# One tile's layers moved four picks up, three of its steps held back behind the expert sums, and one wait added on the weight queue

## The chip, the cores and the metric

One Trainium2 chip, one core of it. The metric is device time in microseconds (us) of one execution. A measurement of this kernel can tell about 0.2% from no change.

## The reference

256 tokens of width 1024 pass through two blocks. The first ends in a retrieval feed-forward: each token sums 128 expert rows (8 heads, 16 picks each), with a dot product against one half of a row and a weighted sum of the other half. The second block is a layer stack (short convolution, memory attention, gate/up/down feed-forward, block attention, the same again, a final norm). Cut to what matters here:

```python
def peer_ffn(h, w_query, sub_keys, expert_u, expert_v):      # per block of 128 tokens
    ...
    u = expert_u[experts]
    vsel = expert_v[experts]
    act = jax.nn.gelu(jnp.einsum('thkd,td->thk', u, hb), approximate=False)
    return jnp.einsum('thk,thkd->td', gate * act, vsel)

def swiglu(h, w_gu, w_down):
    g, u = jnp.split(h @ w_gu, 2, axis=-1)
    return (jax.nn.silu(g) * u) @ w_down

for l in range(DEPTH_2):                                       # second block, two layers
    x = x + (short_conv_mixer or moba_attention)(rms_norm_2(x, norm_mix[l]), ...)
    x = x + mem_cross_attention(rms_norm_2(x, norm_mem[l]), ...)
    x = x + swiglu(rms_norm_2(x, norm_ffn[l]), ffn_w_gu[l], ffn_w_down[l])
```

## The kernel before

The 256 tokens are two tiles of 128. The experts are worked in 256 **picks**, one per step n of a ring: picks 0 to 127 belong to tile 0, picks 128 to 255 to tile 1. A pick is one gather by GpSimd of 128 rows of 8 KB (one row for each partition, 1 MiB in all, L1646) into one of nine places (`SLOTS = 9`); a dot product on VectorE (L2145); gelu, weight and a small diagonal matrix on ScalarE (L1592, L1598, L1605); and its sum on TensorE (L1172). Picks go in pairs, so four matmuls of L1172 (written x8 by the trace, which counts two passes of an f32 matmul) are one pair. The gather of pick n waits until `v_used`, the count of summed picks, has reached n - 8.

Under the second half of the picks TensorE does other work: when tile 0's sums are complete (`add_experts(0)`, L2151 to L2161, on VectorE), tile 0's layers run between the pairs of tile 1. Which step stands before which pair is the table `PICK_WORK`, filled by the loop over `STEPS` from pick `LAYER_FIRST` on. `UNDER_ROWS` are the steps of tile 0 placed there. The rest of them (before: the six down products `dn1` and the final norm) is put between steps of tile 1 after the last pair, by the table `FILLS`, which makes `AFTER_ROWS`. All engines walk the same tables, each doing its own part of a step. On VectorE the dots of a pair stand ahead of its part of the step placed one pair earlier, so a dot can wait behind a product of TensorE.

A product step (`gu1 10`, say: the last of eleven gate/up products of the second feed-forward) is 8 matmuls of 128x512 with one 2 MB block of weights (L1011; down products L1089), after which ScalarE and VectorE empty the bank. A turn (`fturn1 4`) is up to four transposes of 128x128 (L1018). `fturn1 4` turns what `gu1 8` and `gu1 9` made, `fturn1 5` what `gu1 10` made.

SyncE asks for the weight blocks in the order of use (`SEQUENCE`), into a ring of three places (`RING_B = 3`): a block is asked for when the product that used the place three blocks before is done (`wait_released`, L607). So the weights of a step are asked for three products ahead, and gathers and weight blocks share the DMA engines. At the last pairs the order is `gu1 8`, `gu1 9`, `gu1 10` of tile 0, then `dn1 0` of tile 0, then `cin 2` of tile 1.

Of the kernel before, what the change touches and what calls it, by code (L numbers as in the profile page):

```python
# [27 lines left out]
PH, PN, PK = 8, 128, 16  # L28
# [8 lines left out]
SLOTS = 9  # L37
# [160 lines left out]
def memory_steps(l):  # L198

    return [(f"turn mem{l}", 2, 2), (f"root mem{l}", 0, 0), (f"q{l} 0", 7, 2), (f"q{l} 1", 7, 0), (f"qturn{l} 0", 2, 2), (f"scores{l} 0", 4, 2),  # L200
            (f"probs{l} 0", 0, 2), (f"pturn{l} 0", 2, 2), (f"values{l} 0", 4, 2), (f"mo{l} 0", 7, 2), (f"mo{l} 1", 7, 0)]


def feed_steps(l):

    steps = [(f"turn ffn{l}", 2, 2), (f"root ffn{l}", 0, 0)]
    for j in range(11):
        steps.append((f"gu{l} {j}", 7, 0 if j else 2))
        if j >= 2 and j % 2 == 0:
            steps.append((f"fturn{l} {j // 2 - 1}", 1, 0))  # L210
    return steps + [(f"fturn{l} 5", 1, 2)] + [(f"dn{l} {c}", 7, 0 if c else 2) for c in range(6)]
# [4 lines left out]
         + [("turn blk", 2, 2), ("root blk", 0, 0), ("bk 0", 7, 2), ("bk 1", 7, 0), ("bq 0", 7, 0), ("bq 1", 7, 0), ("bv 0", 7, 0), ("rope 0", 0, 0),  # L216
            ("bv 1", 7, 0), ("kturn 0", 2, 2), ("bqturn 0", 2, 0), ("bscores 0", 2, 2), ("bprobs 0", 0, 2), ("bpturn 0", 2, 2), ("bvalues 0", 3, 2),
            ("bo 0", 7, 2), ("bo 1", 7, 0)] + memory_steps(1) + feed_steps(1) + [("final 0", 0, 2)])
LAYER_FIRST, PICK_US = 136, 5.2
UNDER_ROWS, DOWN = [], [f"dn1 {c}" for c in range(6)]  # L220
_at, _load = LAYER_FIRST, float(LAYER_FIRST)
for _w, _us, _lag in STEPS:
    _at = max(_at + _lag, 2 * int(_load // 2))
    _load = max(_load, _at) + _us / PICK_US
    if _w not in DOWN + ["final 0"]:
        assert _at < 256
        UNDER_ROWS.append(_w)
        PICK_WORK.setdefault(_at, []).append("layer 0 " + _w)
FILLS = {"turn conv": ["dn1 0"], "cin 2": ["dn1 1"], "pturn0 0": ["dn1 2"], "bk 0": ["dn1 3"], "bpturn 0": ["dn1 4"], "pturn1 0": ["dn1 5"],
         "gu1 3": ["final 0"]}  # L230
AFTER_ROWS = []
for _w, _us, _lag in STEPS:
    for _fill in FILLS.get(_w, ()):
        AFTER_ROWS += [(0, "gain 0")] * (_fill == "final 0") + [(0, _fill)]
# [58 lines left out]
def unit(name):  # L293
    return [n for n, _ in UNITS].index(name)
# [27 lines left out]
def build_program(nc, a, out):  # L322
    plan = weight_plan(a)
    piece = {}
    for n, (name, i, _) in enumerate(plan):
        piece[name, i] = n

    with ExitStack() as ctx:
# [5 lines left out]
        def sem(name):  # L334
            if name not in sems:
                sems[name] = ctx.enter_context(nc.semaphore(name))
            return sems[name]
# [159 lines left out]
        for n in range(len(plan)):  # L497
            i = n % RING if n < RING_4 else EARLY_PLACES[n - RING_4] if n < RING_4 + len(EARLY_PLACES) else (n - RING_4 - len(EARLY_PLACES)) % RING_B
# [14 lines left out]
        dots_done, v_used = sem("dots_done"), sem("v_rows_used")  # L513
# [43 lines left out]
        def wait_released(eng, n):  # L557

            name, i, _ = plan[n]
            if name == "mod":  # L560
                eng.wait_ge(turn_ready, turn(f"m{i}") + 1)
            elif (name, i) == ("out", 0):
                eng.wait_ge(sem("out_half_used"), 1)
            elif (name, i) in last_unit:
                eng.wait_ge(unit_ready, unit(last_unit[name, i]) + 1)
            else:
                eng.wait_ge(sem("piece_used"), middle.index((name, i)) + 1)
# [9 lines left out]
        @block.sync  # L577
        def _(sp):
            sp.dma_start(keep[:, 0:K_COS], a["keep"][:, 0:K_COS]).then_inc(sem("consts_in"), 16)
            for n, (name, i, parts) in enumerate(plan):  # L580
                if n == 3:
                    sp.dma_start(mem[1], a["ctxT"]).then_inc(sem("ctxT_in"), 16)
                    sp.dma_start(small_rows, a["small_rows"]).then_inc(sem("small_rows_in"), 16)
                    sp.dma_start(keep[:, K_COS:K_END], a["keep"][:, K_COS:K_END]).then_inc(sem("late_consts_in"), 16)
                if n == 5:
                    in4 = piece["in", 4]
                    sp.dma_start(slot8[slot_of[in4]][:, 4:8], plan[in4][2][0][0][:, 4:8]).then_inc(landed[slot_of[in4]], 32)
                    sp.dma_start(s_all[:, 0:2048], a["dist"]).then_inc(sem("dist_in"), 16)
                if n == 8:
                    sp.wait_ge(sem("lam_sums"), 1)  # L590
                    sp.dma_start(x, a["x"][0].rearrange("(t p) d -> p t d", p=P)).then_inc(sem("x_in"), 16)
                if (name, i) == ("wq", 0):
                    sp.wait_ge(unit_ready, unit("c1k1") + 1)
                    sp.dma_start(mem[1], a["skT"]).then_inc(sem("keys_in"), 16)
                if (name, i) == ("mk0", 0):
                    sp.wait_ge(sem("h2_ready"), 4)
                    sp.dma_start(mem[2], a["memT"]).then_inc(sem("mem_in"), 16)
                if user_before[n] is not None:
                    wait_released(sp, user_before[n])
                if n == piece["in", 4]:  # L600
                    sp.dma_start(slot8[slot_of[n]][:, 0:4], parts[0][0][:, 0:4]).then_inc(sem("in4_first_half"), 16)
                    continue
                for src, c0, c1 in parts:
                    dst = ring[:, slot_of[n] * 4096 + c0:slot_of[n] * 4096 + c1]
                    if len(src.shape) == 3:
                        dst = dst.rearrange("p (k n) -> p k n", k=src.shape[1])
                    sp.dma_start(dst, src).then_inc(landed[slot_of[n]], 32 // len(parts))  # L607
            for t in range(NT):
                for u, c in enumerate((slice(0, 512), slice(512, D))):
                    sp.wait_ge(sem(f"tile{t}_done{u}"), 1)  # L610
                    sp.dma_start(out[0].rearrange("(t p) d -> p t d", p=P)[:, t, c], x[:, t, c]).then_inc(sem("stored"), 16)
            sp.wait_ge(sem("stored"), 64)
# [1039 lines left out]
        def _(dve):  # L1652
# [3 lines left out]
            def link(ins):  # L1656

                n_steps[0] += 1
                ins.then_inc(steps, 1)
                dve.wait_ge(steps, n_steps[0])  # L1660
# [195 lines left out]
            for half in range(2):  # L1856
                c = slice(half * 512, (half + 1) * 512)
# [290 lines left out]
            def add_experts(t):  # L2148

                dve.wait_ge(v_used, 128 * (t + 1))  # L2150
                acc = (M, T)[t]  # L2151
                for half in range(2):
                    c = slice(half * 512, (half + 1) * 512)
                    part = (h2[:, 0], expert_part)[t][:, c]
                    if half == 0:
                        link(tt(part, acc[0][:, :], g5row[:, c], ALU.mult))
                    else:
                        for to, at in ((0, 64), (64, 0)):
                            q = tt(part[to:to + 64], acc[1][at:at + 64, :], g5row[at:at + 64, c], ALU.mult)
                        link(q)  # L2160
                    tt(x[:, t, c], x[:, t, c], part, ALU.add).then_inc(experts_added[t], 1)  # L2161
# [14 lines left out]
            def memory_scale(l):  # L2176

                if l:
                    dve.wait_ge(sem("mem_sd"), 1)
                    link(nc.vector.reciprocal(rs_m, rs_m))  # L2180
                for k in range(KC):
                    g = C_MKV + 8 * l + k
                    q = stt(memT[l][:, k], memT[0][:, k], cols[:, g:g + 1], rs_m, ALU.mult, ALU.mult)
                q.then_inc(sem("mem_scaled"), 1)
# [7 lines left out]
                    (2, 0): [lambda: key_copy(0, 5), lambda: key_copy(1, 5)],  # L2192
                    (2, 1): [lambda: key_copy(0, 6), lambda: key_copy(1, 6)], (2, 3): [lambda: key_copy(0, 7), lambda: key_copy(1, 7)],
                    (3, 1): [set_ones], (3, 3): [memory_mean],
                    (4, 0): [lambda: memory_scale(1)], (4, 1): [lambda: memory_scale(0)], (8, 1): [lambda: add_experts(0)]}
            tri = keep[:, K_TRI:K_TRI + P]

            def layer_step(t, step, arg):
# [207 lines left out]
```

## Time and profile before

| | |
|---|---|
| runs | 1719.26, 1721.23, 1718.58 us (median 1719.26) |
| profiled execution, its span | 1719.4 us; the page gives no other time of it |
| TensorE busy | 1520.7 us, 88% |
| VectorE, ScalarE, GpSimd busy | 44%, 29%, 17% |
| bytes moved by DMA | 586.83 MB, 341 GB/s over the span |

Times in the trace run from the span's start. A line of the timeline is a run of like instructions on one engine: start, length, line, what it writes and reads, how many, and in brackets the idle time before it with what ended it. The windows give busy time of each engine in a stretch, the clock granted to TensorE (1.00 is full speed) and the rate of the DMA engines. In the list of DMA queues, q0 carries the gathers and q1 the weight blocks.

### The profile page before, as it was taken

To read this page: it belongs to the slowest core of one execution; us is meant where nothing else is said; L and a number is where in the kernel's file an instruction comes from. 1 tells how busy PE (TensorE), PEld (TensorE's weight loads), DVE (VectorE), ACT (ScalarE), POOL (GpSimd) and SP (SyncE) were. 2 spreads that over 40 slices of the span, in tenths; PEclk is the share of its full clock that TensorE was granted. 3 is DMA by queue.
4 is the path that set the end of the run, shared out by engine and by line. 5 is a ranking of instruction groups with operands and counts; after the bars stand their busy time and mean duration, and the time that the engine had idled before them with its cause. 6 is when DMAs were issued, how large, how long until landed. Compare 5 with 4: busy or idle time off the path is not lost.

```text
span 1719.4 us, 15639 instructions
## 1 busy us (share of the span) xinstructions
PE 1520.7 (88%) x5502; PEld 730.4 (42%) x5502; DVE 752.0 (44%) x1816; ACT 502.0 (29%) x1284; POOL 292.4 (17%) x264
## 2 busy tenths in 40 slices
PE   8999998685489894997999897899999999999998
PEld 5444463462153530333343333443444444455443
DVE  2853178866786566456435436532312100031101
ACT  2412134332433223333443224443412110122210
POOL 0000003434434243223212213321000000000000
PEclk9999999896589896898999998899999999999999
DMA  9736339999999999999999999999876677855774
GB/s 371 257 122 227 140 125 406 403 421 421 421 402 421 421 421 421 399 421 420 415 422 419 422 421 420 413 421 422 347 296 235 259 298 284 306 219 217 289 299 185
DMA packets 94029, 586.83 MB, mean 341 GB/s; under 512 B 6912, under 2 KB 7168, under 8 KB 28288
## 3 DMA queue, kind: packets, MB, share of 16 engines
q1 hardware_dynamic: 56080, 313.19, 46.7%
q0 software_dynamic: 37440, 270.55, 38.1%
q10 hardware_dynamic: 432, 2.10, 0.3%
q8 instruction: 44, 0.72, 0.2%
q14 instruction: 33, 0.27, 0.0%
HBM read 584.76 MB, written 1.05 MB: 341 GB/s over the span
## 4 chain that ended last, share of the span: by engine, by line
PE 71%; DMA 18%; DVE 5%; issue 3%; ACT 2%; POOL 0%; SPq 0%; POOLq 0%; DVEq 0%; ACTq 0%
PE bank L1011 34%; DMA arena<-in_peer_rows,pidx 10%; DMA ring<-in_weights 8%; PE bank L1089 7%; PE bank L701 7%; PE bank L1172 4%; PE bank L779 3%; PE bank L976 2%; DVE arena L2145 2%; PE bank L1018 2%; PE bank L987 2%; PE bank L667 1%; PE bank L756 1%; PE bank L1071 1%; DMA ring<-in_w_mod 1%
## 5 line engine op out<-in xcount | busy, mean ns | idle before, releaser
L1646 POOL DMA_INDIRECT arena<-in_peer_rows,pidx x227 | 257.4, 1134 | 578.2 <-PE bank L1172 531.3
L2145 DVE SCALAR_TENSOR_TENSOR arena<-arena,ring 128x1024 f32<-128x1024 f32 x227 | 273.2, 1223 | 111.9 <-DMA arena<-in_peer_rows,pidx 109.1
L1011 PE MATMUL bank<-ring,arena 128*128 128x512 f32 x736 | 319.4, 593 | 0.0
L1011 PE MATMUL bank<-ring,hT_all 128*128 128x512 f32 x544 | 244.4, 605 | 15.6 <-issue 10.6
L1172 PE MATMUL bank<-arena,keep 128*32 128x512 f32 x908 | 159.8, 704 | 101.1 <-ACT keep L1605 101.1
L1011 PEld LDWEIGHTS bank<-ring,arena 128*128 128x128 f32 x736 | 138.5, 190 | 168.8 <-issue 168.7
L1011 PEld LDWEIGHTS bank<-ring,hT_all 128*128 128x128 f32 x544 | 102.8, 193 | 150.9 <-issue 140.2
L1592 ACT ACTIVATE pf<-pf 128x2 f32<-128x2 f32 x128 | 25.9, 202 | 401.4 <-DVE arena L2145 367.1
L2266 DVE TENSOR_TENSOR x_all<-x_all,bank 128x512 f32<-128x512 f32 x40 | 27.5, 688 | 209.6 <-PE bank L1089 115.8
L1172 PEld LDWEIGHTS bank<-arena,keep 128*32 128x32 f32 x908 | 21.3, 115 | 171.1 <-ACT keep L1605 135.0
L701 PE MATMUL bank<-ring,hT_all 128*128 128x512 f32 x192 | 86.0, 603 | 0.6 <-DVE hT_all L1725 0.6
L1646 POOL DMA_INDIRECT spare<-in_peer_rows,pidx x29 | 32.4, 1118 | 296.9 <-DVE pidx L2068 205.4
L1089 PE MATMUL bank<-ring,arena 128*128 128x512 f32 x176 | 75.9, 592 | 0.0
L2289 DVE SCALAR_TENSOR_TENSOR arena<-bank,stat,arena 128x256 f32<-128x256 f32 x22 | 10.6, 484 | 136.2 <-ACT arena L1550 136.2
L1605 ACT ACTIVATE keep<-keep,pf 128x32 f32<-128x32 f32 x256 | 68.2, 313 | 4.2
L779 PE MATMUL bank<-hT_all,ring 128*128 128x128 f32 (+1 forms) x384 | 61.6, 320 | 3.3 <-DMA ring<-in_weights 2.5
L1089 PE MATMUL bank<-ring,s_all 128*128 128x512 f32 x128 | 58.5, 611 | 6.6 <-DMA ring<-in_weights 6.6
L1598 ACT ACTIVATE pf<-pf,grouped 128x1 f32<-128x1 f32 x256 | 61.4, 287 | 4.4
L976 PE MATMUL bank<-mem_all,ring 128*128 128x256 f32 x256 | 62.6, 402 | 0.0
L779 PEld LDWEIGHTS bank<-hT_all,ring 128*128 128x128 f32 x384 | 55.6, 198 | 12.2 <-issue 5.8
L987 PE MATMUL bank<-ring,mem_all 128*128 128x512 f32 x128 | 58.3, 602 | 0.0
L976 PEld LDWEIGHTS bank<-mem_all,ring 128*128 128x128 f32 x256 | 50.5, 201 | 18.0 <-issue 9.2
(391 smaller groups left out, 1698.2 us busy)
## 6 DMA issues: line engine op xcount, KB each, us to landing
ring<-in_weights SPq DMA_DIRECT2D x122, 2048.0 KB
ring<-in_w_mod SPq DMA_DIRECT2D x12, 2048.0 KB
ring<-in_w_in SPq DMA_DIRECT2D x5, 2048.0 KB
ring<-in_weights SPq DMA_DIRECT2D x8, 1024.0 KB
ring<-in_weights SPq DMA_DIRECT2D x8, 512.0 KB
arena<-in_peer_rows,pidx POOLq DMA_INDIRECT x227
ring<-in_w_in SPq DMA_DIRECT2D x2, 1024.0 KB, 17.6
mem_all<-in_b_mod POOLq DMA_DIRECT2D x3, 512.0 KB, 7.2
```

The source lines that it names most:

```text
L701: m = mm(b[:, :], src[:, k, t * P:(t + 1) * P], slot8[w][:, k], start=(k == 0), stop=(k == KC - 1))
L779: m = mm(b[:, s * n:(s + 1) * n], slot8[w][:, k, c:c + P], hT[:, k, cols_of], start=(k == 0), stop=(k == KC - 1))
L976: m = mm(bk[:, b * TOK:(b + 1) * TOK], slot8[w][:, k, (2 * half + b) * P:(2 * half + b + 1) * P], memT[l][:, k], start=(k == 0), stop=(k = ...
L987: m = mm(b[:, :], memT[l][:, 4 * part + k, t * P:(t + 1) * P], slot4[w][:, k, half * 512:(half + 1) * 512], start=(part == 0 and k == 0), ...
L1011: m = mm(b[:, :], src[:, k], slot8[w][:, k], start=(k == 0), stop=(k == KC - 1))
L1018: i = tr(b[:, c * P:(c + 1) * P], src, ident)
L1089: m = mm(b[:, :], v.fT[k], slot8[w][:, k % 8], start=(k == ks[0]), stop=(k == ks[-1]))
L1172: m = mm(acc[b][r:r + 32, :], diag[n % 8], vslot[n % SLOTS][:, b * 512:(b + 1) * 512], start=(n % 128 < 4), stop=(n % 128 >= 124))
L1598: m = f(pw2[:, c + k:c + k + 1], pgel2[:, c + k:c + k + 1], ACT.Copy, scale=grouped[:, g % 4, i % 4, 1, i // 4:i // 4 + 1])
L1605: f(diag[n % 8], eq32, ACT.Copy, scale=pw2[:, c + k:c + k + 1]).then_inc(sem("diag_ready"), 1)
L1646: nc.gpsimd.indirect_dma_start(out=row_in[n % SLOTS], out_offset=None, in_=a["peer_rows"], in_offset=bass.IndirectOffsetOnAxis(ap=pidx[:, ...
L2145: stt(uslot[n % SLOTS], uslot[n % SLOTS], 1.0, h2g[n % 4], ALU.mult, ALU.mult, accum_out=pact2[:, 16 * (g % 2) + k:16 * (g % 2) + k + 1]). ...
```

## The change

1. `LAYER_FIRST` goes from 136 to 132: every step of tile 0 that stays under the picks stands four picks earlier (the first, `turn conv`, ahead of pick 134 in place of 138).
2. `add_experts(0)` on VectorE, which those steps need, moves from behind the dots of pair 134 to behind those of pair 130.
3. `gu1 10`, `fturn1 4` and `fturn1 5` of tile 0 leave the picks and run after the last pair. The fills between tile 1's steps are dealt out anew: `gu1 10` and `fturn1 4` ahead of tile 1's first turn, `fturn1 5` and `dn1 0` ahead of its `cin 2`, and `dn1 1`, `dn1 2` one place later than before; a place at `gu0 0` is new. The last step of tile 0 under the picks, `gu1 9`, stands ahead of pair 244 in place of pair 248.
4. SyncE waits until 247 picks are summed before it asks for `dn1 0` of tile 0 and, its queue being in order, for all that follows.

```diff
-LAYER_FIRST, PICK_US = 136, 5.2
-UNDER_ROWS, DOWN = [], [f"dn1 {c}" for c in range(6)]
+LAYER_FIRST, PICK_US = 132, 5.2
+UNDER_ROWS, DOWN, HELD = [], [f"dn1 {c}" for c in range(6)], ["gu1 10", "fturn1 4", "fturn1 5"]
...
-    if _w not in DOWN + ["final 0"]:
+    if _w not in DOWN + HELD + ["final 0"]:
...
-FILLS = {"turn conv": ["dn1 0"], "cin 2": ["dn1 1"], "pturn0 0": ["dn1 2"], "bk 0": ["dn1 3"], "bpturn 0": ["dn1 4"], "pturn1 0": ["dn1 5"],
-         "gu1 3": ["final 0"]}
+FILLS = {"turn conv": ["gu1 10", "fturn1 4"], "cin 2": ["fturn1 5", "dn1 0"], "pturn0 0": ["dn1 1"], "gu0 0": ["dn1 2"], "bk 0": ["dn1 3"],
+         "bpturn 0": ["dn1 4"], "pturn1 0": ["dn1 5"], "gu1 3": ["final 0"]}
...
+                if (name, i) == ("dn10", 0):
+                    sp.wait_ge(v_used, 16 * PK - SLOTS)
...
-                    (4, 0): [lambda: memory_scale(1)], (4, 1): [lambda: memory_scale(0)], (8, 1): [lambda: add_experts(0)]}
+                    (4, 0): [lambda: memory_scale(1)], (4, 1): [lambda: memory_scale(0)], (8, 0): [lambda: add_experts(0)]}
```

TensorE at the end of the picks, before: from `fturn1 3` (L1018 x4, ahead of `gu1 9` and pair 248) to the first product after the last pair, `dn1 0` (L1089). Rows of L1172 are pairs.

```order
L1018 MATMUL bank<-keep,s_all 128x128 x4
L1011 MATMUL bank<-ring,hT_all 128x512 x8
L1172 MATMUL bank<-arena,keep 32x512 x4
L1011 MATMUL bank<-ring,hT_all 128x512 x8
L1018 MATMUL bank<-keep,s_all 128x128 x4
L1172 MATMUL bank<-arena,keep 32x512 x4
L1018 MATMUL bank<-keep,s_all 128x128 x2
L1172 MATMUL bank<-spare,keep 32x512
L1172 MATMUL bank<-arena,keep 32x512
L1172 MATMUL bank<-spare,keep 32x512
L1172 MATMUL bank<-arena,keep 32x512 x5
L1089 MATMUL bank<-ring,s_all 128x512 x8
```

The same place in the changed kernel (its lines are two higher: L1174 is the pairs, L1013 and L1091 the products, L1020 the turns), from `fturn1 3` on.

```order
L1020 MATMUL bank<-keep,s_all 128x128 x4
L1013 MATMUL bank<-ring,hT_all 128x512 x8
L1174 MATMUL bank<-arena,keep 32x512 x16
L1174 MATMUL bank<-spare,keep 32x512
L1174 MATMUL bank<-arena,keep 32x512
L1174 MATMUL bank<-spare,keep 32x512
L1174 MATMUL bank<-arena,keep 32x512 x5
L1013 MATMUL bank<-ring,hT_all 128x512 x8
L1020 MATMUL bank<-keep,s_all 128x128 x4
L1020 MATMUL bank<-keep,x_all 128x128 x8
L1020 MATMUL bank<-keep,s_all 128x128 x2
L1091 MATMUL bank<-ring,s_all 128x512 x8
```

Before, `gu1 9` was followed by four pairs (248 to 254) with `gu1 10` and two turns among them; now it is followed by six pairs (244 to 254) with nothing among them, and `gu1 10`, the two turns and tile 1's first turn (x8) follow the last pair.

VectorE around `add_experts(0)`, before (L2145 are dots, L2156 to L2161 are `add_experts(0)`; the rest chooses rows of later picks):

```order
L2009 MAX_INDEX ptop<-pf,s_all 128x8
L2145 SCALAR_TENSOR_TENSOR arena,pf<-arena,ring 128x1024
L2145 SCALAR_TENSOR_TENSOR spare,pf<-spare,ring 128x1024
L2156 TENSOR_TENSOR h_all<-bank,hT_all 128x512
L2161 TENSOR_TENSOR x_all<-x_all,h_all 128x512
L2159 TENSOR_TENSOR h_all<-bank,hT_all 64x512 x2
L2161 TENSOR_TENSOR x_all<-x_all,h_all 128x512
L2014 CAST pf<-ptop 128x32
```

And in the changed kernel (L2147 are the dots, L2158 to L2163 `add_experts(0)`):

```order
L1687 COPY ring<-bank 128x512 x4
L2147 SCALAR_TENSOR_TENSOR arena,pf<-arena,ring 128x1024 x4
L2158 TENSOR_TENSOR h_all<-bank,hT_all 128x512
L2163 TENSOR_TENSOR x_all<-x_all,h_all 128x512
L2161 TENSOR_TENSOR h_all<-bank,hT_all 64x512 x2
L2163 TENSOR_TENSOR x_all<-x_all,h_all 128x512
L2007 MAX pf<-s_all 128x8
```

The work of `add_experts(0)` is the same; it stands two pairs of dots earlier, right behind the dots of picks 128 to 131.

## Rows read from the trace of the kernel before

**Rows 1.** The page: chain that ended last, by engine and line.
```profile
PE 71%; DMA 18%; DVE 5%; issue 3%; ACT 2%; POOL 0%; SPq 0%; POOLq 0%; DVEq 0%; ACTq 0%
```

**Rows 2.** Windows: stretch, busy PE, PEld, DVE, ACT, POOL, then PEclk, DMA share, GB/s.
```profile
900.00:1100.00 200.00, 173.41 (x568) 73.68 (x567) 100.03 (x239) 68.10 (x186) 47.33 (x44) 0.92 1.01 419
1180.00:1225.00 45.00, 43.30 (x129) 17.66 (x128) 11.70 (x23) 21.36 (x42) 5.18 (x5) 1.00 1.01 422
1250.00:1719.00 469.00, 456.75 (x1287) 219.95 (x1286) 70.70 (x159) 76.25 (x161) 0.00 (x0) 1.00 0.70 264
```

**Rows 3.** Timeline of TensorE at the end of the picks.
```profile
1202.32 1.06 PE L1172 MATMUL bank<-arena,keep 128*32 128x512 f32 x8
1203.64 7.13 PE L1011 MATMUL bank<-ring,hT_all 128*128 128x512 f32 x16 [0.25 <-DMA ring<-in_weights]
1210.70 1.06 PE L1172 MATMUL bank<-arena,keep 128*32 128x512 f32 x8
...
1212.19 7.03 PE L1011 MATMUL bank<-ring,hT_all 128*128 128x512 f32 x16
1219.15 1.06 PE L1172 MATMUL bank<-arena,keep 128*32 128x512 f32 x8
1220.15 7.13 PE L1011 MATMUL bank<-ring,hT_all 128*128 128x512 f32 x16
...
1231.97 1.07 PE L1172 MATMUL bank<-arena,keep 128*32 128x512 f32 x8 [1.89 <-ACT keep L1605]
1232.96 7.13 PE L1089 MATMUL bank<-ring,s_all 128*128 128x512 f32 x16
```

**Rows 4.** Timeline of GpSimd: the gathers of picks 253, 254 and 255.
```profile
1204.18 1.19 POOL L1646 DMA_INDIRECT arena<-in_peer_rows,pidx  x1 [14.65 <-PE bank L1172]
1205.67 0.93 POOL L1646 DMA_INDIRECT arena<-in_peer_rows,pidx  x1 [0.30 <-issue]
1212.56 0.94 POOL L1646 DMA_INDIRECT arena<-in_peer_rows,pidx  x1 [5.95 <-PE bank L1172]
```

**Rows 5.** DMA queues in 1106 to 1126: packets, MB, share of 16 engines.
```profile
q0 software_dynamic: 1150, 8.37, 100.7%
```

**Rows 6.** DMA queues in 1203 to 1208.
```profile
q1 hardware_dynamic: 273, 2.11, 101.0%
q0 software_dynamic: 1, 0.00, 0.0%
```

**Rows 7.** DMA queues in 1208 to 1210.
```profile
q1 hardware_dynamic: 62, 0.50, 59.8%
q0 software_dynamic: 42, 0.34, 41.4%
```

**Rows 8.** DMA queues in 1182 to 1200.
```profile
q1 hardware_dynamic: 507, 3.91, 52.1%
q0 software_dynamic: 497, 3.68, 49.1%
```

**Rows 9.** DMA queues in 1223 to 1224, where the gathers' last packets are.
```profile
q1 hardware_dynamic: 49, 0.38, 90.4%
q0 software_dynamic: 10, 0.04, 10.0%
```

**Rows 10.** Timeline of VectorE: the last product's copy and the last dots.
```profile
1227.83 0.48 DVE L2289 SCALAR_TENSOR_TENSOR s_all<-bank,stat,s_all 128x256 f32<-128x256 f32 x1 [5.29 <-ACT s_all L1550]
1228.23 1.22 DVE L2145 SCALAR_TENSOR_TENSOR arena<-arena,ring 128x1024 f32<-128x1024 f32 x1
```

**Rows 11.** Timeline of VectorE at tile 0's first steps.
```profile
671.70 1.22 DVE L2145 SCALAR_TENSOR_TENSOR arena<-arena,ring 128x1024 f32<-128x1024 f32 x1 [1.18 <-DMA arena<-in_peer_rows,pidx]
...
684.12 1.22 DVE L2145 SCALAR_TENSOR_TENSOR arena<-arena,ring 128x1024 f32<-128x1024 f32 x1
...
693.44 0.69 DVE L2206 TENSOR_TENSOR hT_all<-bank,keep 128x512 f32<-128x512 f32 x1
```

**Rows 12.** Timeline of TensorE at tile 0's first steps.
```profile
674.30 1.93 PE L1172 MATMUL bank<-arena,keep 128*32 128x512 f32 x8 [3.27 <-ACT keep L1605]
...
686.72 1.94 PE L1172 MATMUL bank<-arena,keep 128*32 128x512 f32 x8 [5.50 <-ACT keep L1605]
688.59 1.73 PE L1018 MATMUL bank<-keep,x_all 128*128 128x128 f32 x8
...
694.23 16.93 PE L1011 MATMUL bank<-ring,hT_all 128*128 128x512 f32 x32 [2.57 <-issue]
```

**Rows 13.** Chain in order of time, tile 1's last products: start, us, what.
```profile
1659.56 0.44 PE bank L1018 x4
1659.99 13.75 PE bank L1011 x32
...
1674.82 0.44 PE bank L1018 x2
```

## The prediction

> **What bounds the kernel now.** I read the chain of the whole span first [rows 1]: TensorE holds 71% of it and DMA 18%, so there are stages of two kinds. The windows tell them apart [rows 2]. From 900 to 1100 us the DMA engines are full (share 1.01, 419 GB/s) while TensorE is busy 173 of 200 us: under the picks, bytes set the pace. From 1250 to the end TensorE is busy 456.75 of 469 us and DMA 70%: there TensorE sets it. Between them, from about 1203 us, lies a short stretch in which TensorE hardly rests either: 43.3 of 45 us [rows 2]. The end of the kernel is therefore (the moment of the last pair) + (all that is left for TensorE). Before, the last pair ends and `dn1 0` starts at 1232.96 [rows 3], and 1719.4 - 1233.0 = 486.4 us follow. I work out how the change moves both.
>
> The timeline of the last pairs shows what they wait for [rows 3]. Pair 244 is summed at 1202.32, then come `gu1 8`, pair 246, a turn, `gu1 9` (1212.19 to 1219.15), pair 248, `gu1 10`, and the rest. The gathers of 253 and 254 are issued 0.8 us after pair 244 is summed, that of 255 after pair 246 [rows 4].
>
> **Part 1, four picks earlier: a gain of 9.6 us at the last step under the picks.** Tile 0's steps keep their order and the pairs between them, and four gathers fewer go ahead of each. With only gathers in flight, 8.37 MB took 20 us [rows 5], so a gather of 1.049 MB is worth 2.5 us and four are worth 10.0, as long as DMA stays full. At the start VectorE decides instead: it is busy throughout, and the first copy of tile 0 stands behind the dots that begin at 684.12 in place of those that end just ahead of 693.44 [rows 11]. That copy then starts at 684.1 + 1.2 = 685.3, and 1.2 us earlier still, since `add_experts(0)` now fills the wait of 1.18 us ahead of 671.70: 684.1, or 9.3 us earlier. TensorE's own wish would be 12.4 us (688.59 - 676.2, the end of pair 132 in place of that of pair 136) [rows 12]. I take 9.6, between 9.3 and 10.0, and keep 8 and 12.4 as ends. So `gu1 9` should be done at 1219.15 - 9.6 = 1209.6.
>
> **Part 2, the last pairs with nothing between them.** This is where the gain is spent. Behind `gu1 9` there now stand six pairs in place of four. Pair 244, which let the gathers of 253 and 254 go ahead of `gu1 8`, now comes behind `gu1 9`. It ends at 1209.6 + 1.0 = 1210.6, and the first of the last three gathers is issued at 1211.4, where before it was 1204.2: in spite of the 9.6 us gained, 7.2 us later.
>
> Before, from that issue to the last byte of pick 255 it took 19.4 us: issued at 1204.18 [rows 4]; up to 1208 not a byte moves on the gathers' queue, which has one packet, while the weights' queue takes all [rows 6]; in the next 2 us there are 0.34 MB [rows 7]; and the last 0.04 MB pass between 1223 and 1224 [rows 9]. So some 4.3 us to the first byte and 15 us for three gathers, 5 us each. That they take 5 and not 2.5 us is the sharing: with both queues full each gets half, 3.68 MB against 3.91 in 18 us [rows 8]. The new wait does not end this. It opens at 247 summed, which is pair 246, right behind pair 244. SyncE then asks for `dn1 0` and at once for `cin 2`, whose place `gu1 9` has freed. 4 MB of weights so run beside the last three gathers from their first byte on. I take the same 19.4 us: pick 255 has landed at 1230.8. (Alone, the three would need 7.5 us in place of 15; I keep that for a rival.)
>
> From the landing to the last sum: before, the dots of 254 and 255 waited behind the copy of `gu1 10` [rows 10], and the last sums ended 4.7 us after the first of them began. With no product in the way only one dot remains. From the start of the dots at 1228.23, two dots of 1.15 us each end at 1230.55, the sums begin at 1231.97 and end at 1232.96 [rows 3]: so 1.4 us pass on ScalarE and 1.0 us on TensorE. One dot, with some 0.3 us ahead of it for the semaphore (my estimate), makes it 0.3 + 1.2 + 1.4 + 1.0 = 3.9 us. With a slow TensorE the sums take 1.94 in place of 1.07 [rows 12]: 4.8 us. End of the picks: 1230.8 + 4.8 = 1235.6, **2.6 us later than before**.
>
> **Part 3, what is left after the last pair: 7.6 us more.** One product is 13.75 / 2 = 6.9 us, `fturn1 4` 0.44 and `fturn1 5` at most 0.44 [rows 13], and none of them replaces a wait: that stretch is busy to 97% [rows 2]. The moved fills cost nothing. `fturn1 5` needs the copy of `gu1 10`, ready about 1 us behind it, and the turns between them take 0.44 + 0.9 us. `gu1 10` itself covers `add_experts(1)` as `dn1 0` did. The new place ahead of `gu0 0` covers a wait of under 1 us. The blocks asked for late (`dn1 0`, `cin 2`) land by about 1233 (3.2 MB of their 4.2 beside the gathers, the rest at full rate), while `dn1 0` is needed 8.7 us behind the last pair and `cin 2` 15.6 us behind it, so I set the added wait at nothing too. If that cover were gone it would cost up to 5 us, one block at full rate.
>
> **Part 4, the clock: 3.0 us more.** From about 1212 to 1235 TensorE would have only four pairs to sum, with gaps of 5 to 10 us. After a gap of 5.5 us before, a pair took 1.94 us, and the products that followed took 16.93 us for two [rows 12] where two take 13.75 at full clock [rows 13]. The granted clock was 1.00 in the stretch of the last pairs before [rows 2]; it should fall to the lower of its two levels (1.2 of 2.4 GHz) and `gu1 10` should pay the difference of 3.2 us, less a little for the first turns being among the slow work: 3.0. The lower end is nothing, if the clock holds.
>
> **Sum:** 2.6 + 7.6 + 3.0 = 13.2 us, against the profiled execution of 1719.4: 1732.6. The median of the runs is 1719.26, 0.1 lower, so **1732.5 us**, 0.8% slower. With the ends of the unknown terms: shift 12.4, no loss of clock (-2.8 - 3.9) gives 1725.9; shift 8 (+1.6) and two of the last gathers 1 us slower each gives 1736.2.
>
> A rule of the Trainium skill would soften this. The page "DMA: Bandwidth & Descriptors", section "Latency and other measured facts", puts the first byte of a DMA issued by GpSimd at about 1 us. The rows here show 4.3 us for a gather. By the page, pick 255 would land 3.3 us earlier and the sum would be 1729.2.
>
> **Rivals.**
> 1. *The last gathers run alone (faster).* The place is the same: gathers 253 to 255 behind `gu1 9`. If weights asked for at pair 246 start too late to take their share, the three need 7.5 us: pick 255 in at 1211.4 + 4.3 + 7.5 = 1223.2, last pair done 1227.1 at full clock, end -5.9 + 7.6 = +1.7. With the shift of 12.4 it is -1.1, and with a quicker first byte (rival 2) -4.4: 1715. It decides when pick 255 lands before 1221.5 (1233.0 - 7.6 - 3.9), 10.1 us behind the issue of 253. For it speaks that the weights' queue needs time too; against it that it is asked 1 us behind and gave half from the start in [rows 7]. Faster over all: 0.12. The part of it that ends within 0.2%, 1716 to 1722.7: 0.10.
> 2. *The first byte comes sooner.* The gather's 4.3 us could be the price of a queue found busy by 2 MB of weights; where the queues are nearly empty, as they now are behind `gu1 10`'s block, it might be 1 us. The time is 1729, within my range. 0.10, slower.
> 3. *Late blocks.* `dn1 0` or `cin 2` lands late and tile 1 starts behind: up to 5 us on top, 1737.6. 0.08.
> 4. *The forecast* (nothing but the sum, 1725.9 to 1736.2): 0.60.
>
> That the change does not do what it says is ruled out by the order of the instructions.
>
> **How the numbers follow.** Slower by over 0.2%: 0.60 + 0.10 + 0.08 = 0.78; within 0.2% (1715.8 to 1722.7, about what a measurement can tell): 0.10; faster: 0.12. The range leaves out the faster case and most of the late blocks: 1718 to 1736.
>
> **What the changed profile would show.** `turn conv`'s first product at 685 in place of 694.2; `gu1 9` done near 1209.6; a stretch of some 25 us behind it with only pairs and a granted clock of 0.5; the gather of 253 issued near 1211; the last byte of gathers near 1231; `gu1 10` beginning at 1235.6 and taking about 10 us; from there to the end 497 us. I am wrong if gathers 253 to 255 land within 12 us of their issue, if `gu1 9` is done before 1205, or if TensorE keeps its clock.

## The result, and the profile after

The changed kernel takes 1733.15 us (median of 4 runs, 1731.88 to 1734.51), the kernel before 1720.24 (4 runs). The ratio is 1.0074, with a 95% interval of 1.006 to 1.0087: slower by 0.7%. Forecast were 1732.5 us and slower. The profiled execution has a span of 1730.1 us (that same execution is timed at 1731.9), 10.7 more than before. In every run on record whose execution has both figures the timed one is 1.7 to 1.9 us above the span, so the profiled execution before, of 1719.4, stands for about 1721.2 us. It was therefore 1.0 us slower than the median of its four, and that of the changed kernel 1.3 us faster than the median of its own: that is why the spans differ by 10.7 us and the medians by 12.9.

The windows of the changed kernel, with the columns of [rows 2]:

```profile
900.00:1100.00 200.00, 167.37 (x564) 72.59 (x564) 106.45 (x259) 69.92 (x195) 51.21 (x47) 0.94 1.01 419
1180.00:1225.00 45.00, 33.20 (x114) 11.70 (x112) 13.46 (x24) 15.43 (x36) 9.29 (x7) 0.84 0.96 384
1209.00:1234.00 25.00, 7.45 (x48) 0.90 (x39) 9.90 (x17) 6.16 (x22) 5.16 (x3) 0.60 0.76 305
1250.00:1730.00 480.00, 467.46 (x1313) 224.83 (x1311) 72.08 (x161) 76.25 (x161) 0.00 (x0) 1.00 0.70 263
```

The stages on both sides look as before: full DMA under the picks, 97% of TensorE after them. The stretch between them does not. TensorE was busy 43.3 of 45 us there and is now busy 33.2; from 1209 to 1234 it works 7.45 of 25 us, at a mean clock of 0.60, and DMA is not full either.

The timeline of TensorE in that stretch answers to [rows 3] (lines are two higher; the pair between 1215 and 1233 is printed in single rows and left out):

```profile
1201.47 7.03 PE L1013 MATMUL bank<-ring,hT_all 128*128 128x512 f32 x16
1208.43 1.92 PE L1174 MATMUL bank<-arena,keep 128*32 128x512 f32 x16
1213.18 1.28 PE L1174 MATMUL bank<-arena,keep 128*32 128x512 f32 x8 [2.83 <-ACT keep L1607]
1215.48 1.94 PE L1174 MATMUL bank<-arena,keep 128*32 128x512 f32 x8 [1.02 <-ACT keep L1607]
...
1233.05 1.93 PE L1174 MATMUL bank<-arena,keep 128*32 128x512 f32 x8 [7.81 <-ACT keep L1607]
1234.91 8.55 PE L1013 MATMUL bank<-ring,hT_all 128*128 128x512 f32 x16
```

`gu1 9` ends at 1208.4 (before: 1219.15), the last pair at 1234.9 (before: 1232.96). So 10.7 us are gained up to `gu1 9`, and 12.7 are lost between it and the last pair. The gathers say why. GpSimd, as in [rows 4]:

```profile
1210.28 1.19 POOL L1648 DMA_INDIRECT arena<-in_peer_rows,pidx  x1 [6.12 <-PE bank L1174]
1211.77 1.99 POOL L1648 DMA_INDIRECT arena<-in_peer_rows,pidx  x1 [0.30 <-issue]
1214.07 1.98 POOL L1648 DMA_INDIRECT arena<-in_peer_rows,pidx  x1 [0.30 <-issue]
```

They are those of 253, 254 and 255, the first 6.1 us later than before. The chain in order of time then ends the picks:

```profile
1214.07 16.36 DMA arena<-in_peer_rows,pidx
1230.42 0.02 issue
1230.44 1.24 DVE arena L2147 x2
...
1233.05 1.93 PE bank L1174 x8
1234.98 8.48 PE bank L1013 x16
```

Pick 255 has landed at 1230.4, 20.1 us after the issue of 253. The list of DMA queues from 1215 to 1229 shows what passed beside the three gathers, to compare with [rows 8]:

```profile
q1 hardware_dynamic: 390, 3.00, 50.9%
q0 software_dynamic: 390, 2.93, 49.8%
```

Half and half. And from 1211 to 1214, where SyncE had asked for two blocks at 1210.4 and the gathers had not begun:

```profile
q1 hardware_dynamic: 93, 0.76, 85.0%
```

### The profile page after: what moved, and what is told of

Its sections match the earlier page's. It is cut to its first block, busy times and chain, and to the rows that moved or that the text cites. A ratio compares the mean times of both kernels' runs of the same rounds, so it can differ in the third digit from the quotient of the medians.

```text
span 1730.1 us, 15642 instructions
## 1 busy us (share of the span) xinstructions
PE 1521.4 (88%) x5502; PEld 729.3 (42%) x5502; DVE 752.5 (43%) x1816; ACT 502.9 (29%) x1285; POOL 293.4 (17%) x264
## 4 chain that ended last, share of the span: by engine, by line
PE 67%; DMA 23%; DVE 5%; issue 2%; ACT 2%; POOL 0%; POOLq 0%; SPq 0%; DVEq 0%; ACTq 0%
PE bank L1013 33%; DMA arena<-in_peer_rows,pidx 11%; DMA ring<-in_weights 9%; PE bank L1091 7%; PE bank L703 7%; PE bank L1174 4%; PE bank L781 2%; PE bank L978 2%; DMA spare<-in_peer_rows,pidx 2%; PE bank L1020 2%; DVE arena L2147 2%; PE bank L989 1%; PE bank L669 1%; PE bank L758 1%; DMA ring<-in_w_mod 1%
## 5 line engine op out<-in xcount | busy, mean ns | idle before, releaser
L2147 DVE SCALAR_TENSOR_TENSOR arena<-arena,ring 128x1024 f32<-128x1024 f32 x227 | 273.7, 1223 | 131.5 <-DMA arena<-in_peer_rows,pidx 128.6
L1013 PE MATMUL bank<-ring,arena 128*128 128x512 f32 x736 | 319.3, 593 | 0.0
L1013 PE MATMUL bank<-ring,hT_all 128*128 128x512 f32 x544 | 249.2, 615 | 19.3 <-issue 10.5
L1174 PE MATMUL bank<-arena,keep 128*32 128x512 f32 x908 | 161.8, 715 | 104.7 <-ACT keep L1607 104.7
L1013 PEld LDWEIGHTS bank<-ring,arena 128*128 128x128 f32 x736 | 138.6, 190 | 169.1 <-issue 169.0
L1013 PEld LDWEIGHTS bank<-ring,hT_all 128*128 128x128 f32 x544 | 104.7, 197 | 159.3 <-issue 145.4
L1174 PEld LDWEIGHTS bank<-arena,keep 128*32 128x32 f32 x908 | 21.7, 115 | 176.3 <-ACT keep L1607 137.8
L703 PE MATMUL bank<-ring,hT_all 128*128 128x512 f32 x192 | 86.0, 603 | 0.6 <-DVE hT_all L1727 0.6
L1091 PE MATMUL bank<-ring,arena 128*128 128x512 f32 x176 | 75.9, 592 | 0.0
L2291 DVE SCALAR_TENSOR_TENSOR arena<-bank,stat,arena 128x256 f32<-128x256 f32 x22 | 10.7, 484 | 138.4 <-ACT arena L1552 138.4
L1091 PE MATMUL bank<-ring,s_all 128*128 128x512 f32 x128 | 58.4, 610 | 5.1 <-DMA ring<-in_weights 5.1
## 6 DMA issues: line engine op xcount, KB each, us to landing
ring<-in_w_in SPq DMA_DIRECT2D x2, 1024.0 KB, 17.4
```

What stands on the lines that cost most here:

```text
L703: m = mm(b[:, :], src[:, k, t * P:(t + 1) * P], slot8[w][:, k], start=(k == 0), stop=(k == KC - 1))
L1013: m = mm(b[:, :], src[:, k], slot8[w][:, k], start=(k == 0), stop=(k == KC - 1))
L1091: m = mm(b[:, :], v.fT[k], slot8[w][:, k % 8], start=(k == ks[0]), stop=(k == ks[-1]))
L1174: m = mm(acc[b][r:r + 32, :], diag[n % 8], vslot[n % SLOTS][:, b * 512:(b + 1) * 512], start=(n % 128 < 4), stop=(n % 128 >= 124))
L2147: stt(uslot[n % SLOTS], uslot[n % SLOTS], 1.0, h2g[n % 4], ALU.mult, ALU.mult, accum_out=pact2[:, 16 * (g % 2) + k:16 * (g % 2) + k + 1]). ...
```

## The experiments

Profiled executions of kernels that are alike up to pick 240 differ by up to 3.8 us in when they reach tile 0's first product (682.6 in the changed kernel, 686.3 and 686.4 in the first two runs below), so I read each run from three marks of its timeline: the end of `gu1 9`, the end of the last pair, and the end of the span. The last column is the ratio of the run times to those of the kernel before, taken on the same chip. A profiled execution can lie off its median (that of two picks and the wait 2.5 us below, that of two picks without it 2.7 below), so the marks show where time goes and the ratio what a kernel is worth.

| kernel | `gu1 9` ends | last pair ends | between | from there to the end | span | ratio, 95% |
|---|---|---|---|---|---|---|
| before | 1219.2 | 1233.0 | 13.8 | 486.4 | 1719.4 | |
| changed | 1208.4 | 1234.9 | 26.5 | 495.2 | 1730.1 | 1.0074 (1.006 to 1.0087) |
| without the wait | 1211.2 | 1236.7 | 25.5 | 494.5 | 1731.2 | 1.008 (1.0058 to 1.0101) |
| wait for all 256 | 1210.8 | 1228.2 | 17.4 | 494.7 | 1722.9 | 1.0026 (1.0014 to 1.0039) |
| only the four picks | 1206.8 | 1237.3 | 30.5 | 488.0 | 1725.3 | 1.0045 (1.0028 to 1.0062) |
| only held back | 1216.8 | 1226.7 | 9.9 | 495.6 | 1722.3 | 1.0027 (1.0015 to 1.004) |
| three products late | 1216.2 | 1234.8 | 18.7 | 487.2 | 1722.0 | 1.0026 (1.0014 to 1.0037) |
| three products late, the wait | 1214.3 | 1232.1 | 17.8 | 487.6 | 1719.7 | 1.0016 (1.0005 to 1.0028) |
| long fill | 1209.3 | 1245.9 | 36.6 | 493.8 | 1739.7 | 1.0115 (1.0091 to 1.0139) |
| short fill | 1209.2 | 1236.3 | 27.0 | 495.1 | 1731.4 | 1.0079 (1.0064 to 1.0095) |
| two products late, wait for all 256 | 1216.4 | 1225.9 | 9.5 | 495.8 | 1721.7 | 1.001 (1.0001 to 1.0019) |
| two picks and the wait | 1211.0 | 1227.8 | 16.8 | 486.4 | 1714.2 | 0.9987 (0.9978 to 0.9996) |
| two picks, no wait | 1211.4 | 1232.3 | 20.9 | 487.2 | 1719.4 | 1.0018 (1.0009 to 1.0028) |

**The wait taken out.** From the changed kernel:

```diff
-                if (name, i) == ("dn10", 0):
-                    sp.wait_ge(v_used, 16 * PK - SLOTS)
```

> The changed kernel without the new wait on the weight queue. My theory (the late issue of gathers 253 to 255 costs, and their sharing with weights asked for at the same moment): dn1 0 is then asked for at about 1200 and cin 2 at 1208.5, so most of their 4 MB passes while the gathers' queue stands empty (1211 to 1215 in the changed kernel), the last three gathers share only with the rest of cin 2, pick 255 lands near 1223 in place of 1229.9, and the kernel takes 1726 to 1728, 5 to 7 us less than the changed one. Rival (the wait protects the last gathers): without it they share earlier and pick 255 lands later, 1733 or more.

1732.87 us: the same as the changed kernel. My 5 to 7 us did not come; the time is the rival's 1733 within the noise. I had seen that the gathers' queue would be free of weights later on, and indeed from 1224 to 1230 it has the engines nearly alone:

```profile
q0 software_dynamic: 289, 2.08, 83.3%
q1 hardware_dynamic: 32, 0.13, 5.4%
```

But the gathers of 251 and 252, issued at 1204.6, now share with `dn1 0` from 1206 on, so they are late by what is won at the end: from 1206 to 1224 the weights move 4.09 MB beside 3.51 MB of gathers. The two blocks, 4.19 MB, pass ahead of the last byte of pick 255 in both kernels. My theory had left out that gathers ahead of 253 are still in the queue. I took from this run that the bytes asked for ahead of the last gather are what counts; runs below show that this count does not hold in general.

**The wait set to all 256 picks.**

```diff
-                    sp.wait_ge(v_used, 16 * PK - SLOTS)
+                    sp.wait_ge(v_used, 16 * PK)
```

> The changed kernel with the wait set to all 256 picks summed, so that no weight block runs beside the last gathers. My theory: gathers 253 to 255 need 7.5 us in place of 15 from their first byte; pick 255 lands near 1222.3, the picks end near 1227, dn1 0 and cin 2 are asked for then and land 7 and 12 us later, just in time behind gu1 10: 1725 to 1727. Rival (late blocks bound tile 1's start): the blocks come too late and it stays at 1730 or above.

1724.45 us, 0.6 below the range of my theory and 8.7 us below the changed kernel. Between `gu1 9` and the last pair lie 17.4 us in place of 26.5, and what follows is as long as in the changed kernel (494.7 and 495.2): the blocks asked for at the last pair come in time behind `gu1 10`. Its queues from 1217 to 1224 hold nothing but gathers:

```profile
q0 software_dynamic: 339, 2.38, 81.9%
```

This is the clearest price of the sharing: 9.1 us for 4.19 MB of weights (10.0 us by the rate of [rows 5]).

**Only the four picks**, on the kernel before (with `add_experts(0)` moved as in the change):

```diff
-LAYER_FIRST, PICK_US = 136, 5.2
+LAYER_FIRST, PICK_US = 132, 5.2
```

> The kernel before with nothing but the four picks (and the earlier addition of tile 0's expert sums). gu1 10 then stands ahead of pair 246. My theory: the last steps are done 10 us earlier, but gather 255 waits behind gu1 10 and is issued near 1218 in place of 1212.6; the picks end near 1231 to 1232: 1718 to 1720, about the time of before. Rival (the shift is worth its 10 us to the whole): 1710. Rival (the whole loss comes from the shift): 1730.

1728.32 us, 7.8 us slower than before: a miss of some 9 us, on the rival's side that the shift itself costs. I had let gather 255 share with part of one block. In fact three blocks (`dn1 0`, `cin 2`, `cin 4`) are asked for ahead of it, since `gu1 8`, `gu1 9` and `gu1 10` are all done before pair 246 is summed. From 1202 to 1230:

```profile
q1 hardware_dynamic: 803, 6.23, 53.3%
q0 software_dynamic: 755, 5.45, 46.7%
```

6.23 MB are those three blocks nearly whole (6.29 MB). The last pair ends at 1237.3, 4.4 us later than before although `gu1 9` was done 12 us sooner.

**Only held back**: the changed kernel with `LAYER_FIRST` 136, `add_experts(0)` at its old place and no wait.

> The kernel before with nothing but the last gate/up product and its turns held behind the last pair, with the new fills, layers at 136 and no wait. My theory: pick 255 lands as before (1223.7), the last pair ends near 1227.6 since no product stands between, 5.4 us earlier, and 7.6 to 8 us of work follow: 1721 to 1723. Rival (holding is free, since TensorE rested anyway): 1714. Rival (holding is what costs): 1730.

1725.69 us by the median (5.2 above before, 2.7 above my range), by the span 1722.3 (2.9 above). The last pair ends 9.9 us behind `gu1 9` in place of 13.8: the dots no longer wait behind a product. From there to the end it takes 495.6 us in place of 486.4. Holding back costs 9.2 and returns 3.9. My 5.4 for the return was too much. The last dot waits for its gather and not for VectorE:

```profile
1222.22 1.23 DVE L2145 SCALAR_TENSOR_TENSOR arena<-arena,ring 128x1024 f32<-128x1024 f32 x1 [0.93 <-DMA arena<-in_peer_rows,pidx]
```

Pick 255 landed at 1222.2, 5.4 us behind `gu1 9` where I had put it 4.5 behind, and from there the last pair took 4.5 us to its end where I had 3.9; it ran at the lower clock, 1.94 us in place of 1.07.

Taken singly, the shift costs 7.8 us and holding back 5.2, 13.0 together, beside 12.9 for the change. This is no proof that they add up: three blocks are asked for ahead of gather 255 in the first, one in the second, two in the changed kernel.

**The last three products at their old picks**, on the kernel before with the four picks; the second run adds the wait on 247.

```diff
+LATE = ['gu1 8', 'fturn1 3', 'gu1 9', 'gu1 10', 'fturn1 4', 'fturn1 5']
...
-        PICK_WORK.setdefault(_at, []).append("layer 0 " + _w)
+        PICK_WORK.setdefault(_at + 4 * (_w in LATE), []).append("layer 0 " + _w)
```

> The kernel before with the four picks, but gu1 8, gu1 9, gu1 10 and the turns between and behind them left at their old picks (246 to 252), nothing held, no wait. My theory: what the end costs is the number of weight bytes asked for before the last gathers, and products that stand ahead of pairs 240 to 246. Here pairs 240 to 244 follow gu1 7 directly, so gathers 249 to 254 are issued near 1195 to 1200, all three products start about 6 to 8 us earlier than before, and the last pair ends 5 to 8 us earlier with nothing moved behind it: 1712 to 1716. Rival (the shift is worth nothing because the DMA engines are full in any case and the same bytes have to pass): 1719 to 1721. Rival (the shift itself costs, as in e3): 1727.

> The same with the changed kernel's wait on dn1 0 (247 summed). By the byte count the wait keeps back at most one block by a few microseconds, since gather 255 is issued at pair 246 as before: within 2 us of e5, 1711 to 1716. Rival (the wait is a benefit of its own wherever the gathers are late): 3 us or more below e5.

1724.18 us (ratio 1.0026, 1.0014 to 1.0037) and 1723.78 (1.0016, 1.0005 to 1.0028). The pair and the gathers did move as expected (gathers 249 to 254 issued from 1195.1 to 1203.7), the time did not follow and lies 8 us above my range. It is between the rivals, 3 us above the first (the same bytes have to pass) and 3 below the second (the shift costs as before). That the wait would change little, by less than 2 us, came out: 0.4 by the medians. After `gu1 7`, pair 244 waits for its dots until 1198.0, so `gu1 8` begins at 1199.2, only 4.5 us sooner than before, in part at the lower clock (8.59 in place of 7.13 us). The last pair waits 5.9 us for its row, where it waited 1.9 before:

```profile
1199.17 8.59 PE L1012 MATMUL bank<-ring,hT_all 128*128 128x512 f32 x16
...
1232.96 1.94 PE L1173 MATMUL bank<-arena,keep 128*32 128x512 f32 x8 [5.89 <-ACT keep L1606]
```

The chain shows what it waits for, the gather of pick 255, which was issued 3 us sooner than before and lands some 6 us later:

```profile
1209.55 20.79 DMA arena<-in_peer_rows,pidx
1230.34 0.02 issue
```

Only one block, `dn1 0`, is asked for ahead of that gather (at 1207.8); `cin 2` and `cin 4` are asked for at 1216.3 and 1224.3. By the bytes asked for ahead, 3.34 MB of gathers and 2.1 MB of weights from 1210 on, it would land near 1223. The queues from 1210 to 1224 show that the blocks asked for later take their half too:

```profile
q0 software_dynamic: 432, 3.15, 54.1%
q1 hardware_dynamic: 354, 2.77, 47.4%
```

And the gathers' last 0.20 MB take until 1229.9, while the weights' queue moves 2.35 MB. Why this rest is so slow no run here tells.

**The clock.** To see what TensorE's clock costs, small matmuls on constants are put ahead of the last three pairs (work that the output does not use): first too many, then fewer.

```diff
+                for _ in range({250: 15, 252: 40, 254: 60}.get(n0, 0)):
+                    mm(M[0][:, 0:P], ident, ident, start=True, stop=True)
```

> The changed kernel with 15, 40 and 60 small matmuls (128x128, on constants, into a bank nobody reads) ahead of pairs 250, 252 and 254, which adds work that the output does not use. My theory: they keep the clock at its upper level through the wait for the last gathers; the last pair takes 1.07 in place of 1.93 us and gu1 10 6.9 to 7.1 in place of 8.4 us, 2.3 us less in all: 1730 to 1731.5 against 1733. Rival (the clock costs nothing there): 1733 or more.

> The changed kernel with 4, 20 and 28 small matmuls ahead of pairs 250, 252 and 254 (each is two passes of 0.115 us, so 0.9, 4.6 and 6.4 us, which now fit into the waits of 1.0, 5.9 and 7.8 us; work that the output does not use). If the clock is what the last pair and gu1 10 pay for (1.93 in place of 1.07, 8.4 in place of 6.9 us), 2.3 us come back: 1730 to 1731.5 against 1733. If not, 1733.

The first took 1741.75 us: each matmul is two passes, so the fill was twice as long as meant and held up the last pair to 1244.9. As a measurement of the price it serves all the same, since the clock stayed up:

```profile
1231.32 13.66 PE L1170 MATMUL bank<-keep 128*128 128x128 f32 x120
1244.91 1.07 PE L1176 MATMUL bank<-arena,keep 128*32 128x512 f32 x8
1245.91 7.13 PE L1013 MATMUL bank<-ring,hT_all 128*128 128x512 f32 x16
```

The last pair takes 1.07 us in place of 1.93, `gu1 10` 7.13 in place of 8.55: together 2.3 us are the clock's. The second took 1733.51 us, as the changed kernel. It left 3.4 us of idleness ahead of the last pair, which took 1.37 us in place of 1.93, but `gu1 10` took 8.48 us again, so it did not test the fill as meant. Whether a fill of the right length would pay stays open.

**`gu1 8` and `gu1 9` at their old picks, `gu1 10` held, wait for all 256.** From the changed kernel, with `LATE` as above but of `gu1 8`, `fturn1 3` and `gu1 9` alone.

> The changed kernel with gu1 8, fturn1 3 and gu1 9 left at their old picks 246 and 248 and the wait set to all 256 picks summed. My theory (the last gather lands when all bytes asked for ahead of it have passed, and the picks end 4 us later): gathers 249 to 254 are asked for ahead of gu1 8 and no weight bytes beyond gu1 10's block pass ahead of pick 255, so it lands near 1218.5, the picks end near 1223 with a product less to wait for, and 495 us follow: span 1717 to 1719, median 1718 to 1720, up to 2 us below the kernel before. Rival (the kernel is bound by DMA up to the last pick whatever is asked when, so that late weights are only paid later): 1724 or more, as e2.

1722.56 us (1.001, 1.0001 to 1.0019), 2.6 us above the expected range of the median and 10.6 below the changed kernel. Pick 255 lands early, though at 1221.4 and not at 1218.5, and the last pair ends at 1225.9, 7 us ahead of before; but 495.8 us follow, with a `gu1 10` of 9.17 us, in part at the lower clock. What holding back costs eats it.

**Two picks up, nothing held, with and without the wait.** On the kernel before, `LAYER_FIRST` 134, `add_experts(0)` moved as in the change. `gu1 10` then stands ahead of pair 248, behind pair 246, on which gather 255 depends.

> The kernel before with its layers two picks further up (134) in place of four, nothing held, and the changed kernel's wait on dn1 0. Pair 246 then stands behind gu1 9 and ahead of gu1 10. My theory (last landing = bytes asked for ahead of it; TensorE busy meanwhile): gu1 9 is done near 1214, gather 255 is issued near 1216 and lands near 1225, gu1 10 runs beside it and keeps the clock, the last pair ends near 1229 to 1230, 3 to 4 us earlier than before with nothing added behind it: span 1715 to 1717. Rival (any earlier start is given back in full): 1719 to 1721 or more.

> The same without the wait: dn1 0, cin 2 and part of cin 4 pass ahead of gather 255, some 2 MB more than with it, so it lands up to 4 us later than in the run with the wait: 1718 to 1721. Rival (the wait is without effect, as in e1 against the changed kernel): the same time as with it.

1718.49 us (0.9987, 0.9978 to 0.9996) and 1723.96 (1.0018, 1.0009 to 1.0028). Here the wait is worth 5.5 us by the medians and 5.2 by the spans. With it the span is 1714.2 where I had 1715 to 1717; without it the span, 1719.4, is inside my range, but the median 3 us above it. In the kernel with it `gu1 10` runs while the last gather comes in, and the product behind the last pair takes 7.13 us, as at full clock:

```profile
1212.03 7.13 PE L1013 MATMUL bank<-ring,hT_all 128*128 128x512 f32 x16
...
1226.14 1.75 PE L1174 MATMUL bank<-arena,keep 128*32 128x512 f32 x8 [0.61 <-ACT keep L1607]
1227.82 7.13 PE L1091 MATMUL bank<-ring,s_all 128*128 128x512 f32 x16
```

The clock did not hold throughout: the granted clock is 0.54 from 1224 to 1226 and 1.00 again from 1228 on, and the last pair took 1.75 us. Without the wait `gu1 10` stands at the same place, but TensorE then rests 5.2 us ahead of the last pair, and the product behind it takes 7.87 us.

The queues from 1205 to 1210 show what the wait does: with it the gathers of 253 and 254, issued at 1204.4 and 1205.7, have the engines nearly to themselves,

```profile
q0 software_dynamic: 260, 1.87, 94.2%
q1 hardware_dynamic: 22, 0.12, 6.0%
```

and without it, in the same five microseconds, they share:

```profile
q0 software_dynamic: 156, 1.11, 53.3%
q1 hardware_dynamic: 139, 1.01, 48.4%
```

With the wait the last pair no longer waits for a gather. Its chain holds no DMA, only the copy of `gu1 10` and the dots behind it:

```profile
1219.70 0.48 DVE s_all L2291
1220.19 1.14 DVE spare L2147 x2
1221.33 3.45 DVE arena L2147 x6
```

The last pair ends 5.1 us sooner than before (in the fastest of its eleven runs) and nothing is added behind it. It is the only kernel here below the one before; the gain of 2.3 us by the medians is clear of its interval, but barely. What the wait alone would do, with the layers at 136, was not run.

## Why the prediction was right

**Part 1, the shift (forecast 9.6 us).** Tile 0's first product began at 682.6 (forecast 685), and `gu1 9` ended 10.7 us sooner in the profiled execution. Over the six kernels at 132 with the same order up to there it ended at 1208.4, 1211.2, 1210.8, 1206.8, 1209.3 and 1209.2, mean 1209.3; over the two at 136 at 1219.15 and 1216.76, mean 1218.0. That is 8.7 us with a scatter of some 2, so the term holds and no finer than that.

**Part 2, the last gathers (forecast 2.6 us later).** Issue of 253 at 1210.3 (forecast 1211.4), pick 255 landed at 1230.4 (1230.8), last pair done at 1234.9 (1235.6): 1.9 us later than before. The mechanism, that pair 244 behind `gu1 9` delays the last three gathers and that these pass beside two weight blocks, is shown by the run with the wait for all 256, where the blocks stay away and 9.1 us return. I wrote that the new wait "does not end this", which the run without it bears out: 1732.87 against 1733.15. The way of counting in the prediction, half the rate for the gathers as long as both queues have something to move, is right: from 1215 to 1229 they moved 2.93 and 3.00 MB. I missed the run without the wait and the one with the shift alone because I started the count too late, at the first byte of gather 253: in the one the gathers of 251 and 252 were still in the queue when `dn1 0` came, in the other a third block was asked for.

After the first runs I went over to a shorter rule, that the last gather lands when all bytes asked for ahead of it have passed. The runs do not bear it out. Of the weight bytes beyond `gu1 10`'s block the queues show this (what passed is the blocks asked for, at 2.1 MB each, less what the weights' queue still moved of them after the gathers' last byte):

| kernel | MB asked for ahead of gather 255 | MB passed by the gathers' last byte | that last byte |
|---|---|---|---|
| before | 2.1 | 2.5 | 1224.0 |
| changed | 4.2 | 4.2 | 1230.0 |
| without the wait | 4.2 | 4.2 | 1231.8 |
| wait for all 256 | 0 | 0 | 1223.4 |
| only the four picks | 6.3 | 6.3 | 1232.4 |
| only held back | 2.1 | 2.5 | 1221.7 |
| three products late | 2.1 | 5.0 | 1229.9 |
| three products late, the wait | 2.1 | 4.5 | 1227.1 |
| two products late, wait for all 256 | 0 | 0 | 1221.0 |
| two picks and the wait | 4.2 | 2.7 | 1222.7 |
| two picks, no wait | 4.2 | 4.8 | 1227.3 |

The two columns agree within 0.5 MB in seven kernels and part in four. What counts, beside the moment at which the gathers are issued, is how many weight bytes pass while the gathers' queue has something to move, whenever they were asked for.

**Part 3, what is left behind the last pair, and part 4, the clock (forecast 7.6 + 3.0).** From the last pair to the end it took 495.2 in place of 486.4 us: 8.8 for both. Of them 1.4 are the slow `gu1 10` (8.55 against 7.13 at full clock), where I had 3.0, taken from a pair of products which had stayed slow for longer; that is the one term mis-sized by half. The rest, 7.4, is the product with its turns (7.6). The slow last pair, 0.9, was in part 2 and is right. The blocks asked for late cost nothing: with the wait for all 256 the rest took 494.7.

**The sum** was 13.2; the spans differ by 10.7, the medians by 12.9. (The forecast set the span of 1719.4 beside the median of 1719.26 as if they were alike; a span is some 1.8 us below its timed run. Since its 13.2 were in effect added to the median, 1732.5 stands.) The spans leave 2.5 us less than forecast: 1.1 from the shift, 1.6 from the clock, and little from the others. The medians are nearer to 13.2 than the terms are, by luck of the two profiled executions: one lay 1.0 above its median and the other 1.3 below. Executions of one kernel differ by 3 us (the changed one) to 8 us (sixteen runs of the kernel before), so terms that are off by 1 us each can't be told from that.

**The rivals.** The last gathers did not run alone. The first byte did not come sooner than before: gather 253, issued at 1210.3, shows its first bytes at 1215.2 (the queue from 1211 to 1214 holds none), 4.9 us behind its issue where [rows 6, 7] gave 4.3, though the gathers' queue was nearly empty. The rule of the Trainium skill that I set beside it, about 1 us for a DMA issued by GpSimd (page "DMA: Bandwidth & Descriptors", section "Latency and other measured facts"), does not describe these gathers of 128 rows, with a full queue or an empty one. Late blocks cost nothing.

## What to carry to other kernels

When two queues share full DMA engines, each gets half as long as both have something to move. So count the bytes that pass on the other queue until the last gather is in, those asked for after it too. Moving compute earlier also moves its weight requests ahead, and can make the chain end later.

Requests for the next stage can be held back until the last gather is asked for, but a wait that opens with that gather's release was worth something only where the gathers' queue ran empty meanwhile: a shift of two picks cost 3.2 us without the wait and gave 2.3 us with it, and in the changed kernel the same wait gave nothing. Held back until the last sum, the requests cost nothing there and 8.7 us came back. In the one faster kernel a product also stood between the pair that lets the last gather go and the end of the chain, and covered the gather; that this placement is needed was not tested by itself.

Moving work out of a stretch that waits into one that does not costs its full time behind (9.2 us here, with the slower clock) and returned less than half of it (3.9).

## What the runs showed that I had not expected

The same wait was worth 0 us in one order (1732.87 without, 1733.15 with it) and 5.5 us in another (1723.96 and 1718.49). In both orders two blocks are asked for ahead of gather 255 with the wait as without it, so that count does not tell them apart. The bytes that pass do. In the changed kernel all bytes of the last three gathers were still to come when the wait opened, and both blocks passed beside them, 4.2 MB as without it. With two picks the gathers of 253 and 254 went out 6.5 to 7.7 us ahead of the opening at 1212.1 and passed nearly alone; their queue was then empty from 1214.9 to 1217.4, where weights passed at no cost to a gather, and only gather 255 had to share. 2.7 MB passed in place of 4.8. The difference of 2.1 MB is 5.0 us by the rate of [rows 5], and the gathers' last byte came 4.5 us sooner.
